# A decoder kernel: past key and value pages read by four sequences abreast on TensorE, and one state store issued later

## The reference

```python
# each sample b has 4 pages of 128 past tokens, found through page_table
kg = cache_k[li][page_table].reshape(db, past_len, SB_HEADS, SB_HEAD_DIM)
vg = cache_v[li][page_table].reshape(db, past_len, SB_HEADS, SB_HEAD_DIM)
...
z = jnp.einsum('bqhd,bkhd->bhqk', qb, kb).astype(jnp.float32) * scale + bias
log_1m = jnp.where(mask, jax.nn.log_sigmoid(-z), 0.0)
log_w = jax.nn.log_sigmoid(z) + lax.cumsum(log_1m, axis=3, reverse=True) - log_1m
w = jnp.where(mask, jnp.exp(log_w), 0.0)
outs.append(jnp.einsum('bhqk,bkhd->bqhd', w.astype(vb.dtype), vb))
...
u_ext = jnp.concatenate([pool_buf.astype(u.dtype), u], axis=1)   # the last 15 pooling inputs, then the new one
return y, k, v, u_ext[:, -POOL_BUF:]                             # the new state: again the last 15
```

## Time and profile before

| | |
|---|---|
| device time, median of 3 runs | 2439.23 us |
| lowest and highest of these | 2437.92 and 2440.74 us |
| the profiled execution's own time | 2440.66 us |
| its span in the profile | 2439.0 us |
| PE busy | 2391.9 us (98%), 18794 records |
| PEld busy | 2184.2 us (90%) |
| DVE busy | 1242.9 us (51%) |
| ACT busy | 996.7 us (41%) |
| chain that ended last, by engine | PE 88%, DVE 5%, ACT 3%, DMA 2%, issue 2% |

### The profile page before, as it was taken

The page is one execution under the profiler, slowest core; times in us unless marked ns, Lnnn a source line. Parts: engine busy times, 40 slices in busy tenths (PEclk is TensorE's granted clock), DMA queues, the critical chain, the costliest instruction groups (busy, mean ns, idle before and its releaser), DMA issues.

```text
span 2439.0 us, 43786 instructions
## 1 busy us (share of the span) xinstructions
PE 2391.9 (98%) x18794; PEld 2184.2 (90%) x18794; DVE 1242.9 (51%) x1725; ACT 996.7 (41%) x1399; POOL 114.9 (5%) x232
## 2 busy tenths in 40 slices
PE   6999999999999999999999999999999999999998
PEld 5999999965599999999999999887777999999998
DVE  4533336755576332357533346745555658633245
ACT  4522234635456222346522245523322546522243
POOL 0000000121100000000000000011222100000000
PEclk8999999999999999999999999999999999999999
DMA  8555455775536644565755345654555456643254
GB/s 282 178 165 173 129 183 178 257 217 126 191 115 213 199 160 135 178 210 176 242 160 169 117 156 184 189 165 156 166 171 168 131 172 184 190 142 92 86 178 154
DMA packets 122658, 417.09 MB, mean 171 GB/s; under 512 B 23386, under 2 KB 27610, under 8 KB 122210
## 3 DMA queue, kind: packets, MB, share of 16 engines
q1 hardware_dynamic: 89538, 302.08, 39.2%
q10 hardware_dynamic: 17568, 61.87, 7.5%
q0 software_dynamic: 15360, 50.34, 6.4%
HBM read 390.84 MB, written 23.41 MB: 170 GB/s over the span
## 4 chain that ended last, share of the span: by engine, by line
PE 88%; DVE 5%; ACT 3%; DMA 2%; issue 2%; SPq 0%; POOLq 0%; POOL 0%; ACTq 0%; DVEq 0%
PE PS L2008 71%; PE PS L1403 3%; PE PS L1942 3%; PE PS L1972 2%; PE PS L1333 1%; DVE WL L2292 1%; ACT WH L2120 1%; DMA AFIRST<-in_w_ada 1%; PE PS L769 1%; PE PS L1287 1%; PE PS L1318 1%; PE PS L1328 1%; PE PS L1299 1%; ACT Y L2169 1%; PE PS L772 1%
## 5 line engine op out<-in xcount | busy, mean ns | idle before, releaser
L2292 DVE TENSOR_TENSOR WL<-RAW,WH 128x1024 fp32r<-128x1024 f32 (+1 forms) x478 | 633.1, 1325 | 677.2 <-ACT WH L2120 676.5
L2008 PE MATMUL PS<-HH,WH 128*128 128x260 f32 x3432 | 799.6, 286 | 3.0 <-DVE QKVS L1097 1.0
L2008 PE MATMUL PS<-HH,WL 128*128 128x260 f32 x3432 | 786.0, 282 | 0.0
L2008 PE MATMUL PS<-HL,WH 128*128 128x260 f32 x3368 | 769.6, 283 | 0.0
L2120 ACT ACTIVATE WH<-RAW 128x1024 fp32r<-128x1024 f32 (+1 forms) x478 | 542.4, 1135 | 402.7 <-PE PS L2008 275.3
L2008 PEld LDWEIGHTS PS<-HH,WH 128*128 128x128 f32 x3432 | 569.2, 188 | 35.3 <-issue 26.6
L2008 PEld LDWEIGHTS PS<-HH,WL 128*128 128x128 f32 x3432 | 569.3, 188 | 0.0
L2008 PEld LDWEIGHTS PS<-HL,WH 128*128 128x128 f32 x3368 | 557.5, 188 | 0.6 <-issue 0.2
L2008 PE MATMUL PS<-GH,WH 128*128 128x260 f32 x1408 | 386.3, 284 | 0.1
L2008 PE MATMUL PS<-GL,WH 128*128 128x260 f32 x1408 | 384.2, 283 | 0.0
L2008 PE MATMUL PS<-GH,WL 128*128 128x260 f32 x1408 | 383.5, 283 | 0.0
(11 more groups left out here) (338 smaller groups left out, 2313.7 us busy)
## 6 DMA issues: line engine op xcount, KB each, us to landing
RAW<-in_w_in SPq DMA_DIRECT2D x236, 512.0 KB, 3.6
RAW<-in_w_out SPq DMA_DIRECT2D x120, 704.0 KB, 4.0
AW<-in_w_ada ACTq DMA_DIRECT2D x114, 512.0 KB, 4.5
RAW<-in_w_odd SPq DMA_DIRECT2D x60, 512.0 KB, 3.6
RAW<-in_w_odout SPq DMA_DIRECT2D x30, 512.0 KB, 3.7
RAW<-in_w_even SPq DMA_DIRECT2D x28, 512.0 KB, 4.2
KV<-in_v_pages POOLq DMA_DIRECT2D x32, 256.0 KB, 4.9
SR<-in_ret_past POOLq DMA_DIRECT2D x32, 256.0 KB, 4.0
```

The source lines that it names most:

```text
L2008: last = nc.tensor.matmul(ps[:, x, 0:HT], w[:, k * P:(k + 1) * P], src[k0 + k][:, x, :], start=(begin and t == 0), stop=(end and t == 2))
L2292: nc.vector.tensor_tensor(low_, RAW[:, from_:from_ + w], high_.bitcast(F32), ALU.subtract).then_inc(lo_done, 1)
```

## The change

**Key pages.** A call of `scores_past` now takes four sequences with two pages each, in all four column groups, as 16 matmuls of 128 x 16 by 128 x 256 in place of 8 of 128 x 512. Sequences 0 to 3 are calls 0 and 1, sequences 4 to 7 calls 2 and 3. **Value pages.** A call of `values_past` takes the same four sequences with two pages each, still 8 matmuls of 128 x 8 by 128 x 512, but now four column groups abreast. **Buffers.** A buffer of four pages now holds two pages of each of two sequences. The number of pages, their size, the order of buffers and the semaphore counts on which POOL waits stay as they were.

**Order.** Calls 0 and 1 of `scores_past` both stand behind step 21, call 2 in the middle of step 25, call 3 in the middle of step 26. The clearing of their PSUM bank moves in DVE's program from step 21 to step 19.

**Stores.** The samples' pooling state is stored in head 1, behind that head's modulation weights, and counts on `late_out`. The prompt's pooling state goes first and has its own semaphore `pool_out`, on which DVE now waits in head 2 in place of all the stores. ACT waits for all of them before evout.

```diff
@@ -598,8 +598,8 @@
                 if i == 3:
                     sp.wait_ge(ev_act, EV_FULL)
                     sp.wait_ge(ev_dve, EV_FULL)
-                    for dst, src in ((k_t[:, 0:4 * SEQ], KP[:]), (k_t[:, 4 * SEQ:4 * SEQ + 32], QKVS[:, 4:8, :]),
-                                     (pool_p, UP[:, :, SEQ + 1:SEQ + 16]), (pool_n, US[:, :, :, 1:16])):
+                    sp.dma_start(pool_p, UP[:, :, SEQ + 1:SEQ + 16]).then_inc(pool_out, 16)
+                    for dst, src in ((k_t[:, 0:4 * SEQ], KP[:]), (k_t[:, 4 * SEQ:4 * SEQ + 32], QKVS[:, 4:8, :])):
                         sp.dma_start(dst, src).then_inc(out_done, 16)
                     sp.wait_ge(vp_evac, 4)
                     sp.dma_start(v_t, VP[:]).then_inc(out_done, 16)
...
+                        if h == 1:
+                            sp.dma_start(pool_n, US[:, :, :, 1:16]).then_inc(late_out, 16)
...
                 for t in range(4):
-                    for b, n in zip((2 * q, 2 * q + 1), bufs):
-                        c = 96 * t + 24 * (b % 4) + 8 * (b // 4)
-                        last = nc.tensor.matmul(PS[2][32 * (b % 4):32 * (b % 4) + 16, 0, :], QBM[:, c:c + 16],
-                                                PAGE[n][:, :, t * P:(t + 1) * P], start=(b < 4 and t == 0),
-                                                stop=(b >= 4 and t == 3), tile_position=(0, 32 * (b % 4)))
+                    for g in range(4):
+                        c = 96 * t + 24 * g + 8 * (q // 2)
+                        last = nc.tensor.matmul(PS[2][32 * g:32 * g + 16, 0, keys], QBM[:, c:c + 16],
+                                                PAGE[bufs[g // 2]][:, 2 * (g % 2):2 * (g % 2) + 2, t * P:(t + 1) * P],
+                                                start=(q == 0 and t == 0), stop=(q == 3 and t == 3),
+                                                tile_position=(0, 32 * g))
                 last.then_inc(kv_used, 1)
 
             def values_past(q):
@@ -631,13 +635,13 @@
                 pe.wait_ge(pz_ok, 1) if q < 2 else pe.wait_ge(os_ok, 1)
                 for n in range(2):
                     pe.wait_ge(kv_in[n], 64 * (q + 3))
-                for p in range(PAGES):
-                    for n in range(2):
-                        b = 2 * q + n
-                        c = p * P + 32 * (b % 4) + 8 * (b // 4)
-                        last = nc.tensor.matmul(PS[3][32 * (b % 4):32 * (b % 4) + 8, 1, :], ZW[:, c:c + 8],
-                                                PAGE[n][:, p, :], start=(p == 0), stop=(p == PAGES - 1),
-                                                tile_position=(0, 32 * (b % 4)))
+                for k in range(2):
+                    p = 2 * (q % 2) + k
+                    for g in range(4):
+                        c = p * P + 32 * g + 8 * (q // 2)
+                        last = nc.tensor.matmul(PS[3][32 * g:32 * g + 8, 1, :], ZW[:, c:c + 8],
+                                                PAGE[g // 2][:, 2 * (g % 2) + k, :], start=(p == 0),
+                                                stop=(p == PAGES - 1), tile_position=(0, 32 * g))
                 last.then_inc(kv_used, 1)
 
...
-                if half == 1 and i in (22, 23, 24, 25):
-                    scores_past(i - 22)
+                if (i, half) == (21, 1):
+                    scores_past(0)
+                    scores_past(1)
+                if half == 0 and i in (25, 26):
+                    scores_past(i - 23)
...
                     if t == 1:
-                        dve.wait_ge(out_done, 96)
+                        dve.wait_ge(pool_out, 16)
...
+                if i == 19:
+                    dve.wait_ge(mod_ready, 4)
+                    nc.vector.memset(PS[2][:, 0, :], 0.0).then_inc(z_zero, 1)
                 if i == 21:
                     pack_samples()
-                    dve.wait_ge(mod_ready, 4)
-                    nc.vector.memset(PS[2][:, 0, :], 0.0).then_inc(z_zero, 1)
...
-            def pages(src, b, n):
-
-                for p in range(PAGES):
-                    at_ = b * PAGES + p
-                    row = pool.value_load(PT[0:1, at_:at_ + 1], min_val=0, max_val=PHYS - 1)
-                    pool.dma_start(PAGE[n][:, p, :], src[bass.ds(row, 1)].rearrange(
-                        "o p n -> (o p) n")).then_inc(kv_in[n], 16)
+            def pages(src, q, n, buf):
+
+                for e in range(2):
+                    for k in range(2):
+                        at_ = (4 * (q // 2) + 2 * n + e) * PAGES + 2 * (q % 2) + k
+                        row = pool.value_load(PT[0:1, at_:at_ + 1], min_val=0, max_val=PHYS - 1)
+                        pool.dma_start(PAGE[buf][:, 2 * e + k, :], src[bass.ds(row, 1)].rearrange(
+                            "o p n -> (o p) n")).then_inc(kv_in[buf], 16)
 
```

More of the change, by code:

```diff
@@ L948, in even_act @@
             table(ROOT_SET)
-            act.wait_ge(out_done, 96)
+            act.wait_ge(out_done, 64)
+            act.wait_ge(pool_out, 16)
+            act.wait_ge(late_out, 16)
             for q, (n, hs) in enumerate(STEPS["evout"]):
@@ L1222, in even_pool @@
                 for n in range(2):
-                    pages(k_pages, 2 * q + n, 2 * (q % 2) + n)
+                    pages(k_pages, q, n, 2 * (q % 2) + n)
             pool.wait_ge(kv_used, 3)
             for n in range(2):
-                pages(v_pages, n, n)
+                pages(v_pages, 0, n, n)
             for h in range(2):
@@ L1235, in even_pool @@
                 for n in range(2):
-                    pages(v_pages, 2 * t + 2 + n, n)
+                    pages(v_pages, t + 1, n, n)
         od_in = sem("od_in"); dec_in = sem("dec_in")
@@ L1930, in _ @@
                 sp.wait_ge(q, 16 * PHASE * RH // NBUF)
-            sp.wait_ge(y_out, 16 * 5)
+            sp.wait_ge(late_out, 16 * 6)
         @block.tensor
```

10 lines of the change are left out of this document (6 added, 4 removed).

## The result

The changed kernel takes **2444.9 us** (median of 13 executions, 2443.3 to 2448.4), the kernel before, measured beside it, 2439.2 (13 executions, 2435.4 to 2444.9). The ratio is 1.0024, 95% interval 1.0016 to 1.0031: 5.7 us, or 0.24%, slower. The forecast was 2432.3 in a range to 2437.5, so it was wrong in sign too.

What follows compares the result with a forecast made beforehand. PE was taken to bound the kernel (88% of the chain that ended last). Keys 4.2 us plus values 2.7, stores 0, gave 6.9 us off the median 2439.23, so 2432.3 us, range 2429.5 to 2437.5.

Steps and rivals of the forecast that it cites:

- What four abreast gives: Past's key and value matmuls on PE: four column groups run at two's pace, saving 1.77 us a call, 14.2 over eight.
- each group streams at about half the pace: Past's matmuls: 512 columns last 0.40 us untiled, 0.59 in a column group, so four abreast give about 2x, not 4x.
- Keys, calls 0 and 1: Both key calls behind step 21: 3.5 us saved, a new 3.2 us stall before the first pooling product, 0.3 remaining.
- DVE's part does not move: Before the first pooling product: step 23 still ends at 519.5, DVE's differences still at 522.64, so PE waits 3.2 us.
- Calls 2 and 3: Key calls in steps 25 and 26: 1.8, 2.0 of page wait and 1.8 gained, 1.65 lost before the second score.
- Values: The four value calls: 0, 0.6, 0.4 and 1.7 us gained, together 2.7 of 7.1.
- head 0 stall: After value call 0, PE waits for DVE's softplus; the call gains 0 and the stall grows to 2.7 us.
- Call 1's 0.6: Second value call: only 0.6 us gained, since DVE's softplus cannot start before ACT's logarithm ends at 613.53.
- The stores: Samples' pooling state stored in head 1 beside call 1's value pages: cost 0 at best, 4.2 us at worst, taken as 0.
- The clock: Rival, new stalls at 519.5 and 586.5: a fall costs 1.7 to 3.4 us, two give 2435.7 to 2439.1; chance 0.30.
- late pages: Rival, heads 1 and 2: value pages or AW landing as long as 15.7 us cost 4.2, giving 2436.5; chance 0.12.
- slower-side rival: Value call 1: pages or AW 24 us late plus a 3.4 us clock fall give 2448; gains gone at 18.4; chance 0.05.

Runs made afterwards that it cites:

- e7: The kernel before with only the new page layout (four sequences abreast, two pages each), calls and stores at their old places: 2435.9 us, ratio 0.9987.
- e1: The changed kernel with the store of the samples' pooling state put back behind the keys' stores: 2439.3 us, ratio 0.9997.
- e4: e1 with call 1 of the key pages taken back to its old place behind step 23: 2436.4 us, ratio 0.9986.
- e10: The changed kernel with the samples' pooling state stored one head later, behind head 2's modulation blocks: 2440.6 us, ratio 1.0002.
- e6: The changed kernel with half of the samples' pooling state stored behind the keys' stores, the other half in head 1: 2437.8 us, one execution.
- e9: The changed kernel with six needless matmuls before the second value call, where PE waited for a page: 2446.6 us, ratio 1.0023.
- e3: The changed kernel with six needless matmuls ahead of the first pooling product, in the stall behind step 23: 2443.5 us, ratio 1.0012.
- e5: e4 with five needless matmuls in head 0's stall, ahead of the second sums: 2436.4 us, ratio 0.9983.
- e11: The changed kernel with needless matmuls in all three long stalls (first pooling product, head 0's second sums, second value call): 2445.8 us, ratio 1.0025.

## Why the prediction was wrong

**What four abreast gives: right, but for a wrong reading beside it.** Calls start the next work 1.74 (keys) and 1.72 us (values) after their start, forecast 1.77. What the prediction says against the 4x of the Trainium skill (TensorEngine Tiling, Overview and Performance Considerations) does not hold. The record of 512 columns that it calls untiled, 0.40 us, is of WL and HH, which are float32r in the kernel and show one record a matmul:

```profile
L2304 DVE TENSOR_TENSOR WL<-RAW,WH 128x1024 fp32r<-128x1024 f32 x8 | 9.8, 1220 | 9.0 <-ACT WH L2132 9.0
```

The past's matmuls are float32 with two records each. An untiled float32 matmul of 512 columns (SB by TRI) goes from 587.24 to 588.20, so 0.96 us. In column groups, two abreast took 3.54 us for eight matmuls of 512 columns, 0.44 each, and four abreast take 1.72, 0.22 each. The last is 4.5 times the untiled pace, so this trace reaches the page's 4x, and the prediction's "each group streams at about half the pace" was an error. It changed no term of the sum, because the turn was taken from the ada rows.

**Keys, calls 0 and 1: right, blind to the alternative.** The stall came as 3.13 us (forecast 3.2). From the mark behind step 21 the product starts after 12.7 us and not 13.0, so 0.3 earlier as forecast. "DVE's part does not move" held for the two calls behind step 21. That the same calls in their old places start it after 11.0 was not seen; it is what e7 has over e1.

**Calls 2 and 3: right.** The page wait of 1.88 went, the ZA wait is 1.53 (forecast 1.65 in all). In e1, whose clock held through this stretch, the second score comes 41.1 us behind the mark and before 45.1: 4.1 us gained, forecast 4.2.

**Values: right but for one term.** The head 0 stall is 2.69 (forecast 2.7). In e4, whose clock held throughout, the stretch from the second score to the evout mark is 102.9 us and before 104.9: 2.0 gained, forecast 2.7. Call 1's 0.6 did not come: behind it PE waits 1.15 us for DVE before the next sums and 2.10 in place of 1.49 before the next score, together the whole 1.77. Call 2 gave 0.35 (forecast 0.4) and call 3 1.7, as forecast. With the keys of e1, the change's own gain is 6.1 us, forecast 6.9.

**The stores: the first step that failed.** The prediction worked out both ends, 0 and 4.2 us, from a landing of 15.7 us and 10.3 us of room, and took 0, "in the old stretch a store of 1 MB and key pages ran too". The landing was 16 us and the room 10.4, so the wait was 5.5. The end that was set aside was the right one, and the row behind it was this very store. What hid it in the old stretch was not that the pieces are harmless there. Before too, the eight value pages issued in 530 to 560 took 13.6 us to land in the median and 15.7 at most; the first of them were wanted only at 583.74. Issues from 530 to 560 of before (KB each, median us to landing):

```profile
KV<-in_v_pages POOLq DMA_DIRECT2D x8, 256.0 KB, 13.6
```

The store's place costs 5.6 us (after less e1) and 4.3 (after less e10).

**The clock: the second.** The prediction had it as a rival with 0.30 and a price of 1.7 to 3.4 a fall, 2435.7 to 2439.1 for two. A fall's missing time of 3.4 us was right for both falls in after; in other profiles it is often 1.7. But late pages, the clock and the forecast were set up as cases that exclude each other, and a long stall makes both: the page wait was itself the longest stall and brought a fall with it. Only the slower-side rival had the two together, with 0.05, and wanted a landing of over 18.4 us. It did not need that: two falls and the wait at 16 us were enough. At the first place the 2.05 us before call 3 had "left the clock at 1.00", which was one execution. The clock in a stall is not a property of the kernel alone: e1 and e6 have the same 3.13 us stall as after, and in their profiles no fall there.

**The sum again, with what was measured.** The change's own gain of 6.1 us is taken from e1's keys and e4's values, where the clock held. Against it stand, in after's profile, the first fall with 2.7 us (43.8 less 41.1), and 5.9 us from the second score to the evout mark (108.7 less 102.9), where the page wait of 5.5 with its fall of the clock stands. Together the stage is 2.5 us longer, which is what the two marks show. How the 5.9 divide between wait and clock is not shown: PE also waits 0.58 us for a block of AW at 640.82, and later waits for DVE get shorter, from 2.10 to 1.44 us before the next score.

The stage is not the whole of the time. In the two profiles after is 3.3 us longer: 2.5 in the stage, 1.4 behind it, and 0.6 less ahead of it. The medians differ by 5.7. The rest is open: it lies in what one execution doesn't tell, among it how often the clock falls: the mean clock over all executions is 0.9962 before and 0.9932 after. In the same way e1's stage is 4.3 us shorter than before's and its median only 1.1 lower, at a mean clock of 0.9949. e1 was expected at 2435 and e4 at 2432 to 2433. Both came about 4 us higher although the waits went as expected, and one profile each doesn't tell why. e7's profile (2431.05 us) was the fastest of its 11 executions, and lies 4.9 under their median.

**By parts, from medians:** the layout alone -4.7 (e7), the new places +3.4 (e1 less e7), the store +5.6 (after less e1), in all +4.3; the direct comparison gave 5.7. Each has an uncertainty of 2 to 4 us by its interval, so the new places' +3.4 is not clear of noise by itself.

## What to carry to other kernels

A store of thousands of small pieces is priced by what it does to the loads beside it, not by its bytes or by who waits for it: put it where the next load that someone needs is far off, and if its landing is known from one place, use that number at the next. When a helper's work gets shorter, look at what it covered: put the shorter pieces one each into the gaps that the other engines leave and not two together in front of one. A stall can cost its length and then the clock, so a late transfer and a fall of the clock belong in one case of a forecast and not in two. And compare two profiles from a mark right ahead of the change: the first 500 us, the same in all kernels here, put them up to 3.4 us apart.

## What the runs showed of the hardware

Whether the granted clock falls in a short stall varies from one execution to the next. The same 3.13 us stall, behind the same instructions on PE, left 3.4 us of clock missing in after's profile, 1.7 in those of e9 and e10, and none in those of e1 and e6. The stall of 1.53 us before the second score is followed by a fall in e3, e5, e6 and e10 and by none in after, e1, e4, e9 and e11. Every fall between 500 and 664 began in a stall of 1.5 us or more or within 2 us behind it, and left 1.7 or 3.4 us missing. Before itself, with no stall over 1.9 us in the stretch, spreads over 2434.9 to 2446.9 us in 81 executions, and its mean clock from 0.995 to 0.997.

Float32 matmuls with 8 or 16 stationary columns, four column groups abreast, ran at 0.22 us for one of 512 columns, where an untiled one took 0.96.

A store of 4096 pieces, 240 KB in all, takes 20.7 us to land, of which 10 at 13 to 27 GB/s (e10), and value pages of 256 KB that run with it land in 14.7 us (median of eight) and not 4.7. AW's blocks of 512 KB beside it took 8.9 and not 4.5.
